# Three stages of a two-layer attention/mLSTM step: a gate unit split in two, one product moved up, seven row places

## What is computed

```
h = rmsnorm(x, w) * (1 + scale) + shift              # both layers
# layer 0: 16 query heads of 64, 4 key heads, sink logit, window of 128 either side + 256 cached keys
q, g, k, v = split(h @ w_in);  q, k = rope(q), rope(k)
o = softmax_with_sink(q k^T / 8) v
x = x + gate * ((o * silu(g)) @ w_out)
# layer 1: 8 heads of 128, two directions, chunked matrix memory
q, k, v, o, g, gates = split(h @ w_in)
w = exp(a - mt);  w0 = exp(a0 - mt)                  # a, a0, mt: rows made from the gates
num = ((q k^T) * w) v + w0 * (q C);  den = max(|sum(s) + w0 * (q n)|, exp(-mt))
y = (((num / den forward) + (num / den backward)) * sigmoid(o) * silu(g)) @ w_out
x = x + gate * y;   out = rmsnorm(x, final_w)
```

## Time and profile before

| | us |
|---|---|
| median of 3 runs | 2644.57 |
| lowest and highest | 2643.67, 2651.73 |
| the profiled execution, whole | 2647.19 |
| its span in the trace | 2645.3 |
| mean granted PE clock, as a share of full speed | 0.994 |

### The profile page before, as it was taken

One profiled execution on the slowest core, in us unless ns is written; L12 is line 12 of the kernel. 1 busy time (PEld: TensorE's weight loads), 2 busy tenths in 40 slices (PEclk: granted clock), 3 DMA queues, 4 the chain that ended last, 5 costly groups with the idle time before them and its releaser, 6 DMA issues.

```text
span 2645.3 us, 49651 instructions
## 1 busy us (share of the span) xinstructions
PE 2575.9 (97%) x18563; PEld 2252.8 (85%) x18563; DVE 1200.6 (45%) x3271; ACT 897.7 (34%) x2118; POOL 628.3 (24%) x816
## 2 busy tenths in 40 slices
PE   6999999999999999999999999999999999999998
PEld 3678898888888887887899999999999999998786
DVE  5764646556464665552242333414243332415533
ACT  4453626536363563223222131313122131313211
POOL 1412132131222213331021130403022130403232
PEclk8999999999999999999999999999999999999999
DMA  9702121030211215331131221303132121316443
GB/s 362 242 25 74 38 69 61 27 90 18 70 53 55 70 48 180 130 128 59 31 63 59 39 84 24 106 17 86 41 61 65 39 84 19 88 39 178 148 148 105
DMA packets 188732, 219.62 MB, mean 83 GB/s; under 512 B 27248, under 2 KB 133504, under 8 KB 186576
## 3 DMA queue, kind: packets, MB, share of 16 engines
q1 hardware_dynamic: 180880, 192.26, 25.5%
q10 hardware_dynamic: 7616, 24.22, 2.4%
HBM read 178.27 MB, written 38.17 MB: 82 GB/s over the span
## 4 chain that ended last, share of the span: by engine, by line
PE 58%; issue 1%; DVE 1%; POOL 1%; DMA 0%; SPq 0%; ACT 0%; POOLq 0%; ACTq 0%; DVEq 0%
PE psum L549 12%; PE psum L551 12%; PE psum L550 12%; PE psum L2495 2%; PE psum L2560 2%; PE psum L2045 2%; PE psum L2047 2%; PE psum L2046 2%; PE psum L2563 2%; PE psum L1580 2%; PE psum L1582 2%; PE psum L1581 2%; PE psum L2543 1%; PE psum L2486 1%; PE psum L2450 1%
## 5 line engine op out<-in xcount | busy, mean ns | idle before, releaser
L549 PE MATMUL psum<-h_hi,m_w_lo 128*128 128x384 f32 (+1 forms) x1600 | 594.1, 371 | 1.1 <-ACT gt_nat L1493 1.1
L551 PE MATMUL psum<-h_hi,m_w_hi 128*128 128x384 f32 (+1 forms) x1600 | 573.7, 359 | 0.0
L550 PE MATMUL psum<-h_lo,m_w_hi 128*128 128x384 f32 (+1 forms) x1600 | 573.0, 358 | 0.0
L549 PEld LDWEIGHTS psum<-h_hi,m_w_lo 128*128 128x128 f32 x1600 | 301.3, 188 | 26.0 <-issue 1.7
L551 PEld LDWEIGHTS psum<-h_hi,m_w_hi 128*128 128x128 f32 x1600 | 300.5, 188 | 26.9
L550 PEld LDWEIGHTS psum<-h_lo,m_w_hi 128*128 128x128 f32 x1600 | 301.6, 189 | 22.5
L549 PE MATMUL psum<-h_hi,attn_w_lo 128*128 128x384 f32 (+1 forms) x800 | 293.1, 366 | 2.3 <-DVE attn_w_lo L534 2.3
L551 PE MATMUL psum<-h_hi,attn_w_hi 128*128 128x384 f32 (+1 forms) x800 | 285.8, 357 | 0.0
L550 PE MATMUL psum<-h_lo,attn_w_hi 128*128 128x384 f32 (+1 forms) x800 | 285.5, 357 | 0.0
L951 ACT ACTIVATE arena<-arena,stats 128x640 f32<-128x640 f32 (+2 forms) x272 | 213.4, 785 | 74.1 <-DVE stats L1032 73.1
L1032 DVE CUSTOM_DVE_ANT_0 arena<-psum,wmask,stats 128x640 f32<-128x640 f32 (+2 forms) x256 | 206.0, 839 | 59.1 <-PE psum L1243 58.4
(11 more groups left out here) (335 smaller groups left out, 4639.2 us busy)
## 6 DMA issues: line engine op xcount, KB each, us to landing
m_bc<-gate_rows_mlstm SPq DMA_DIRECT2D x128, 256.0 KB, 3.3
m_w_raw<-in_mlstm_w_in SPq DMA_DIRECT2D x40, 512.0 KB, 4.7
h_full<-gated_output SPq DMA_DIRECT2D x29, 512.0 KB, 3.9
gated_output<-gT SPq DMA_DIRECT2D x8, 1088.0 KB, 5.2
layer_output<-xb_out ACTq DMA_DIRECT2D x17, 512.0 KB, 2.7
h_hi_full<-layer_output SPq DMA_DIRECT2D x17, 512.0 KB, 4.8
out<-h_hi_full ACTq DMA_DIRECT2D x17, 512.0 KB, 4.9
attn_w_raw<-in_attn_w_in SPq DMA_DIRECT2D x16, 512.0 KB, 6.5
```

Of the source, the lines that this page charges most:

```text
L549: pe.matmul(out, self.lo[:, k, :], E.h_hi[:, k, tok], start=(k == 0), stop=False)
L550: pe.matmul(out, self.hi[:, k, :], E.h_lo[:, k, tok], start=False, stop=False)
L551: ins = pe.matmul(out, self.hi[:, k, :], E.h_hi[:, k, tok], start=False, stop=(k == KT - 1))
```

## The change

Four edits of order, and two more buffers; no arithmetic is added or removed.

1. **Attention, unit 4.** Its slices 0 to 5 stay ahead of turn(0); slices 6 and 7 (6 matmuls) go behind turn(1), ahead of scores(3). ACT takes its tanh between the two exponentials of block 2, DVE the `(tanh + 1) * g` behind the rest copy of block 1, ahead of the maxima of block 3. In the last pass the rounding of the weight slice moves behind the copies of block 15.
2. **First output stage, DVE.** The gate product of tile 2 comes before `og_low(4)` and `low(0)`, and the modulation of tile 0 before all three.
3. **Last mLSTM head.** Seven row places: two more lie in the raw weights, which are free by then. The output weights are issued after row 6, the first part of the last stage's input after row 9. DVE does the first two score products before the gate steps of group 4, and PE's first product waits for one gate step less.
4. **Towards the last stage.** ACT rounds four pieces of the output weights inside the last head; the stores and loads for tiles 1 and 2 are issued ahead of six other loads of 512 KB; in tile 0 PE lags four slices behind, not two.

```diff
@@ ACT, attention
-                        for g in range(NG):
+                        for g in range(NG - 1):
+                            gate_tanh(g)
...
+                            turned_pairs(s - 2)
+                            if s < NT:
+                                exponential(s, 0)
+                                if s == 2:
+                                    gate_tanh(NG - 1)
+                                exponential(s, 1)
+                                sink_exp(s)
+                            if last and s == NT:
...
@@ DVE, attention
+                            if s == 3:
+                                ungated(NG - 1)
@@ PE, attention
-                    unit(kv, m, 4)
+                    unit(kv, m, 4, 0, KT - 2)
...
+                        if s == 2:
+                            unit(kv, m, 4, KT - 2, KT)
@@ DVE, first_output
+            if n == 2:
+                og_low(4)
+                low(0)
...
-            if n + 3 < NT:
-                og_low(n + 3)
             if n == 1:
                 modulate(0)
-                low(0)
+            elif n + 3 < NT:
+                og_low(n + 3)
@@ FinalOutput
+    EARLY_W = 4
...
-        LAG = 2
+        LAG = 4
@@ phase_mlstm
+        rows_of = [bc, bc + [weights[0][:, 4 * j:4 * j + 4, :] for j in range(2)]]
...
                         if last and c == NB:
+                            sp.wait_ge(J.s_lo, at(2 * (5 * MH)))
+                        if last and c == NB + 2:
                             sp.wait_ge(J.s_unit, at(MH * NU - 4))
                             F.sp_weights(sp)
+                        if last and c == NB + 5:
                             sp.wait_ge(J.s_unit, at(MH * NU))
                             sp.wait_ge(s_ogst, at(16 * (MH - 1)))
                             F.load_og(sp, 0, 0, KT - 1)
...
-                        sp.wait_ge(s_num, at(h * NT + max(c - NB + 1, 0)))
+                        sp.wait_ge(s_num, at(h * NT + max(c - len(rows_of[last]) + 1, 0)))
...
                         for n in range(1, 3):
                             F.load_og(sp, n, KT - 1, KT)
+                        F.sp_rows(sp)
...
+                        if last and s in (4, 6, 8, 10):
+                            F.act_early_w(act, s // 2 - 2)
...
+                    EARLY_S = 2 if last else 0
...
+                        if m == 3 and g == NG - 1:
+                            for s in range(EARLY_S):
+                                weighted_scores(s)
...
-                                pe.wait_ge(s_relD, at(h * NG + NG))
+                                pe.wait_ge(s_gd, at(h * NG + NG - 1))
+                            if c == 1:
+                                pe.wait_ge(s_gd, at(h * NG + NG))
```

More of the change, by code:

```diff
@@ L1943, in pool, with w_high, act_early_w @@
                 self.og_high(pool, n + 3)
+    EARLY_W = 4
+    def w_high(self, act, i):
+        k, half = i // 2, i % 2
+        act.copy(self.w_hi[half][:, k, :], self.w_raw[half][:, k, :]).then_inc(self.s_whi, 1)
+    def act_early_w(self, act, i):
+        act.wait_ge(self.s_w[i % 2], 16)
+        self.w_high(act, i)
     def act_first_og(self, act, i, gT):
@@ L1961, in act @@
         E = self.E
-        for half in range(2):
-            act.wait_ge(self.s_w[half], 16)
-        for k in range(KT):
-            for half in range(2):
-                act.copy(self.w_hi[half][:, k, :], self.w_raw[half][:, k, :]).then_inc(self.s_whi, 1)
+        for i in range(self.EARLY_W, 2 * KT):
+            self.w_high(act, i)
         for n in range(NT):
@@ L2087, in phase_mlstm, with ring, rows_loaded @@
             "backward_state", "state_stored", "gate_tanh", "gate_steps"))
-        s_bc = [sem(f"rows_loaded{x}") for x in range(NB)]
+        s_bc = [sem(f"rows_loaded{x}") for x in range(NB + 2)]
+        def ring(last, c):
+            return c % len(rows_of[last])
+        def rows_loaded(h, last, c):
+            x = ring(last, c)
+            per = -((x - NT) // NB) if x < NB else 0
+            return at(h * (16 * per) + 16 * (c // len(rows_of[last]) + 1))
         (s_E, s_qw, s_W, s_S, s_P, s_num, s_den, s_rec, s_part, s_hm, s_hT, s_og, s_ogst) = (sem(x) for x in (
@@ L2341, in head @@
                             value_tiles(h + 1, g, value_bank(g))
+                        if last and s == 4:
+                            act.wait_ge(J.s_unit, at(MH * NU))
                         if last and 11 <= s < 14:
```

56 lines of the change are left out of this document (29 added, 27 removed).

## The result

| | before | changed |
|---|---|---|
| median, us | 2649.48 (6 runs) | 2631.94 (6 runs) |
| lowest and highest | 2643.67, 2651.73 | 2631.45, 2636.58 |
| profiled execution, whole | 2647.19 | 2632.24 |
| its span | 2645.3 | 2630.4 |

The ratio of the runs is 0.9947, with a 95% interval of 0.9937 to 0.9957, so about 14.0 us (11.4 to 16.7) less. The forecast was 17.0 us less, 0.9936 of the time before: the right sign, and about 3 us too much.

What follows compares the result with a forecast made beforehand. PE, busy 97% of the span, was taken as the bound, with gains only where it stands still or runs at the lower clock. 6.3 + 0.7 + 4.7 + 5.3 = 17.0 off 2644.57 gave 2627.6 us, range 2623 to 2635.

Steps and rivals of the forecast that it cites:

- Part A: Attention, unit 4 split: six matmuls fill the hole before scores(3), 0.79 us a pass, 6.3 us (2.4 to 7.6) over 8.
- The last pass: Last attention pass: moving ACT's rounding behind the copies of a late block saves PE 0.7 us (0 to 1.0).
- some 0.3: Last attention pass: the output stage's first product then waits some 0.3 us for the moved rounding.
- Part B: First output stage: PE's idle before tile 2's transposes goes, 3.1, and its low clock, 1.6: 4.7 us (0.5 to 5).
- tile 2 is normalised at 1047.1 to 1048.4: First output stage, DVE: with the new order tile 2 is normalised then, against 1051.5 before.
- Part C: Last head and last stage: head ends 4.5 us earlier, tile 1 starts 5.3 us earlier (wider bounds 3 to 7).
- I take 2424.1: Last head: when row 7 reaches POOL, between 2423.6 (its own time) and 2425.0 (queue of weights).
- part of the first idle: Last head: some of PE's 1.65 us idle, added to POOL's 2.7 and 1.27 for row 16 some 5.0 earlier.
- R2: Rival, chance 0.10: output stage only passes its stall on or low clock stays; gain there 0.5 to 3.1, total 2629 to 2632.
- R1: Rival, chance 0.15: ACT makes turn(2) wait each pass; attention gain 0 to 3 us, not 6.3, total 2631 to 2634.
- R3: Rival, chance 0.07: last head bound by weights landing late or rows behind them; gain there 0 to 2, total 2631 to 2633.
- R5: Rival, chance 0.02: slower, DVE's `ungated(4)` waits for ACT's tanh; 2.3 us late a pass loses all 17.0.

Runs made afterwards that it cites:

- a_only: The kernel before with only the attention edits of the change: ratio 0.9979 (0.9970 to 0.9989), medians 2641.7 and 2647.32 us.
- w_split: Changed kernel, second half of output weights issued behind row 8, last stage's input one row later, four early ACT roundings four steps later: last head 30.00 us.
- w_late: Changed kernel, second half of output weights issued behind the last row, one early ACT rounding instead of four: last head 24.53 us, to tile 1 14.98.
- tanh_late: Changed kernel with ACT's tanh of unit 4 behind both exponentials of block 2: attention 837.03 us, against 834.96 in the changed kernel.

## Why the prediction was right and where not

- **Part A, 6.3 us: right, 6.1 with the last pass in it.** The 0.79 a pass was 0.79 (PE's timelines, mean of seven passes; 0.75 to 0.86), the changeovers, the tanh's place and the margin on DVE (0.20 for 0.17) as worked. turn(2) did wait 0.17 for ACT, which the sum had at nothing; it was covered, since 0.19 of idle stood behind it before.
- **The last pass, 0.7: wrong, -0.2.** The step that failed is "some 0.3" for the first product's wait. I took that wait without following ACT's list to its end: behind the copy of block 15 stood the rounding, 1.05, and PE wanted it 0.65 before its end; and turn(16)'s copy now stood behind it too.
- **Part B, 4.7: the gain was 3.2, and half of that not by the reason given.** The wait went from 2.91 to 1.21, 1.7 us and not 3.1. The step that failed is "tile 2 is normalised at 1047.1 to 1048.4": `low(0)` and POOL's sum were priced at their durations apart. The chain I moved forward brought them to the same moment. The row that would have told it (2.02 against 1.23) stood in front of me, and I used it for Part C alone. The other 1.5 us is the clock, and it did come; but a_only, with a wait of 2.85 and a clock of 1.00, shows that the wait before the change need not cost it. That this trace of the kernel before had the low stretch is luck for the forecast; it should have been in the range, not in the sum. (The Trainium skill, *TensorE: Matmul & The Clock Gate*, "What's actually happening", says that what the gate looks at is "free-running", not tied to the kernel's own events. I drew on the page only for how busy PE had been. That one wait of 2.9 us brings the low clock and another doesn't would fit the part that I left aside; no run here tests it.)
- **Part C, 5.3: 3.9.** The head's end was put 4.5 sooner and came 3.93. The step that failed is "I take 2424.1" for row 7, which is 7.8 us behind the last unit matmul: it came 8.8 behind it, at the bound that the queue of weights sets (w_split and w_late, with half of the weights ahead of it, have it at 5.6). Two rows at 1.37 and the wait of 1.27 are 4.0, and POOL shows row 16 3.9 sooner; the "part of the first idle" added on top wasn't there. Then 0.8 was to come behind the head, and it was 0.0: DVE lost 1.7 where I took about 1.0 from a range of 0 to 1.6 (two remainders took 1.53 and 1.52, over the 0.7 that I had named as a sign of error), and that ate up what came from the wait for POOL (0.94, gone) and by `og_low(1)` that runs undisturbed (tile 1 starts 1.3 behind its start, before 2.1).
- **Rivals.** R2 came true in part (B within 0.5 to 3.1 if the clock is left out). R1 did not: ACT's chain held. R3's size, 0 to 2 us for C, did not come; its mechanism, rows behind the weights, is in the changed kernel as POOL's wait of 6.64 and in w_split as one of 5.67. R5 is real, as tanh_late shows, at 0.26 us a pass for half a microsecond of lateness.
- **The range.** 2623 to 2635 holds the median of the runs, 2631.94; on the footing of the ratio, 0.9947 of the later median of before (2649.48), it is 2635.4, just outside. The bound of 2635 was put on rivals one by one; that each of three terms is a little short at the same time was the likelier way to miss.

## What to carry to other kernels

Read a stage's gain between the same matmuls of two traces: it is good to 0.3 us in the attention and the output stage and to 0.9 in the last head, where medians of runs wander by 5, once the granted clock of each stretch has been read beside it. When a reordering brings a DVE step with two inputs from SBUF next to a GpSimd step, price them one after the other, not side by side; here a step that reads PSUM stood beside the sum without loss, and giving the rounding to ACT freed DVE. And an operation moved behind another on its engine has to be followed to its own consumer: a wait that leaves one matmul may stand at the next.

## What was not expected

- DVE and POOL held each other up in both directions in one place: 3.42 for 1.23 and 3.37 for 2.39 us. Two roundings on POOL, of the kind that takes 1.04 alone, cost DVE 0.85 each.
- The lower clock behind a wait is not a function of the wait's length: after 2.85 us none, after 1.87 and 2.91 us 1.5 to 1.7 us lost. In a_only's last head it followed an idle of 2.41 us. What decides it was not settled here.
- A half of the weights (2 MB) issued behind the last rows was 11.5 us from issue to its first use (w_late); one such half in front of a row of 256 KB let POOL wait 5.67 us (w_split).
- The first 160 us of the span vary by 4.5 us between traces (first scores at 156.41 to 160.91), in part by PE's waits (27.5 to 31.3 us), in part by stretches of low clock. That this is most of the spread between runs of one kernel is likely, but there are no stages of the unprofiled runs to show it.
